# Two transformer blocks in one kernel: the small loads, the output product, the router and the context's channels in another order

## The reference

```python
# first block
h = rmsnorm(x, g_mix)
q_a, k_a, v_a, cx, cb, cc, q_m, gate_logits = split(h @ w_in)      # 768 x 6, 512, 3072 columns
...                       # rope and dilated attention, a convolution, attention to 256 memory rows
merged = sum(sigmoid(gate) * (branch @ w_proj))                    # three branches
x = x + merged @ w_out                                             # 1024 x 1024
h2 = rmsnorm(x, g_ffn)
pg = softmax(h2 @ w_rg + b_rg)                                     # 4 groups, the best one
pe = softmax(the 8 logits of that group)                           # the best 2 experts
weights = pg_top * pe_top / sum(pe_top)
x = x + sum over the picks of weights * (silu(h2 @ w_gate[e]) * (h2 @ w_up[e])) @ w_down[e]   # 32 experts, 512 wide
# second block, with a context of 256 further tokens
mod_c, mod_l = silu(c_ctx) @ w_ada + b_ada, silu(c) @ w_ada + b_ada
pc = project(ctx * (1 + scale_c) + shift_c)     # w_in: channels, conv of 5 taps, silu; gates
pl = project(x * (1 + scale_l) + shift_l)
y, o = SSD scan and gated delta rule, both directions, the context first, its state handed to x
x = layer_norm(alpha * x + g1 * (concat(y, o) @ w_out))
x = layer_norm(alpha * x + g2 * swiglu(x * (1 + scale2) + shift2))
```

## Time and profile before

| | |
|---|---|
| median of three runs | 1622.11 us |
| the three runs | 1621.21, 1622.11, 1624.6 us |
| profiled execution, own time | 1621.47 us |
| its span in the trace | 1619.7 us |
| TensorE's mean granted clock | 0.977 |
| TensorE busy | 1510.5 us |
| VectorE busy | 775.4 us |
| ScalarE busy | 377.3 us |
| GpSimd busy | 217.1 us |
| moved by the DMA engines | 370.46 MB, mean 229 GB/s |

### The profile page before, as it was taken

The page is one execution under the profiler, slowest core; times in us unless marked ns, Lnnn a source line. Parts: engine busy times, 40 slices in busy tenths (PEclk is TensorE's granted clock), DMA queues, the critical chain, the costliest instruction groups (busy, mean ns, idle before and its releaser), DMA issues.

```text
span 1619.7 us, 23438 instructions
## 1 busy us (share of the span) xinstructions
PE 1510.5 (93%) x9510; PEld 1071.4 (66%) x9510; DVE 775.4 (48%) x1583; ACT 377.3 (23%) x842; POOL 217.1 (13%) x364
## 2 busy tenths in 40 slices
PE   7999999999899888779998989999899999999997
PEld 4888655554677565456675768875568774788843
DVE  5557311432544425514445347777987761210156
ACT  1001154321421112223332232133444320100000
POOL 3000000000000000123134010001265612400000
PEclk9999999999999989989999999999999999999999
DMA  9444432653699999999999943342153242444351
GB/s 323 160 156 156 156 104 104 219 194 152 263 406 406 407 406 405 416 418 416 407 417 415 381 165 129 131 156 104 53 221 105 105 156 104 156 156 156 109 203 52
DMA packets 124208, 370.46 MB, mean 229 GB/s; under 512 B 10555, under 2 KB 26565, under 8 KB 107589
## 3 DMA queue, kind: packets, MB, share of 16 engines
q1 hardware_dynamic: 118352, 362.04, 59.1%
q0 software_dynamic: 1280, 6.29, 1.1%
q10 hardware_dynamic: 4469, 0.62, 0.3%
HBM read 367.89 MB, written 1.05 MB: 228 GB/s over the span
## 4 chain that ended last, share of the span: by engine, by line
PE 74%; DMA 10%; DVE 7%; ACT 3%; issue 2%; POOL 2%; ACTq 1%; SPq 1%; DVEq 0%; POOLq 0%
PE psum L2309 49%; PE psum L684 8%; PE psum L2104 4%; DMA ring<-in_w_up 4%; DMA ring<-in_w_in 4%; PE psum L2303 3%; DMA ring<-in_w_down 2%; PE psum L2126 2%; PE psum L2088 1%; PE psum L2145 1%; ACTq L2616 1%; POOL area L1901 1%; PE psum L2475 1%; PE psum L2447 1%; POOL area L1902 1%
## 5 line engine op out<-in xcount | busy, mean ns | idle before, releaser
L2309 PE MATMUL psum<-area,ring 128*128 128x256 f32 (+1 forms) x1952 | 423.2, 376 | 6.4 <-DMA ring<-in_w_in 4.7
L2309 PEld LDWEIGHTS psum<-area,ring 128*128 128x128 f32 x1952 | 361.0, 192 | 57.7 <-DMA ring<-in_w_in 7.0
L2309 PE MATMUL psum<-ring,area 128*128 128x512 f32 (+1 forms) x976 | 386.6, 552 | 9.6 <-ACT area L2600 5.0
L2309 PEld LDWEIGHTS psum<-ring,area 128*128 128x128 f32 x976 | 186.1, 193 | 192.3 <-issue 181.2
L684 PE MATMUL psum<-area 128*128 128x128 f32 x1216 | 152.6, 284 | 15.9 <-DVE area L1493 11.7
L684 PEld LDWEIGHTS psum<-area 128*128 128x128 f32 x1216 | 144.5, 196 | 31.9 <-DVE area L1493 13.1
L2600 ACT ACTIVATE area<-psum 128x512 f32<-128x512 f32 (+1 forms) x103 | 57.0, 586 | 424.5 <-PE psum L2309 354.2
L2104 PE MATMUL psum<-ring,area 128*32 128x256 f32 x1792 | 111.1, 394 | 16.4 <-DMA ring<-in_w_up 16.4
L2309 PE MATMUL psum<-area 128*128 128x256 f32 (+4 forms) x442 | 99.5, 375 | 3.7 <-DVE area L1582 2.6
L2303 PE MATMUL psum<-const,area 128*128 128x128 f32 (+2 forms) x507 | 79.0, 281 | 20.5 <-DVE area L2259 5.5
L2104 PEld LDWEIGHTS psum<-ring,area 128*32 128x32 f32 x1792 | 56.9, 112 | 60.9 <-issue 28.9
(11 more groups left out here) (364 smaller groups left out, 1562.3 us busy)
## 6 DMA issues: line engine op xcount, KB each, us to landing
ring<-in_w_in SPq DMA_DIRECT2D x28, 2048.0 KB, 8.6
ring<-in_w_gate SPq DMA_DIRECT2D x56, 1024.0 KB, 13.5
ring<-in_w_up SPq DMA_DIRECT2D x56, 1024.0 KB, 15.6
ring<-in_w_down SPq DMA_DIRECT2D x48, 1024.0 KB, 14.3
ring<-in_w_ada SPq DMA_DIRECT2D x12, 2048.0 KB, 7.9
area<-in_w_down SPq DMA_DIRECT2D x16, 1024.0 KB, 17.7
ring<-in_w_in SPq DMA_DIRECT2D x12, 1024.0 KB, 12.0
ring<-in_w_out SPq DMA_DIRECT2D x6, 2048.0 KB, 7.7
```

Source lines behind the costliest of these rows:

```text
L2309: last = nc.tensor.matmul(dst, lhs(k), rhs(k), start=first and k == 0, stop=final and k == count - 1)
```

## The change

Six edits, all of order:

1. ScalarE issues the first eight small loads, then does the copies of in0 and the first copies of groups 0 and 1, and then issues the other eight small loads.
2. `v_rest` is put in bank 0 by name, outside the rotation.
3. The output product goes by token tiles: both weight halves for token tile 0, then both for tile 1, with tile 0's eight transposes of h2 between the last two. VectorE and ScalarE follow: add, square sum, root, scale and transposes' copies for each token tile by itself. `wo0` is released after the third tile, not after the second.
4. The context's channel 0 moves from ahead of the h2 transposes to behind the router's transposes.
5. VectorE does the rank's copy and the places before the picks' weights, not behind them.
6. `CTX_GAP` goes from 3 to 1: channels 1 and 2 are woven in among the experts, and the plan of the stage and the list of the weights are made anew from that.

```diff
-CTX_GAP = 3
+CTX_GAP = 1
...
             w, = unit("in4")
-            dst = open_tile("v_rest")
+            dst = open_tile("v_rest", (0,))
...
-            for i in range(2):
-                w, = unit(f"wo{i}")
-                for t in range(NT):
-                    tokens_by_weights(("wo", i, t), mergedT, t, w)
-                used(f"wo{i}")
-
-
-            columns_landed(pe, 0)
-            decay_columns_pe(pe, 0, open_tile, product)
-            context_channel_pe(pe, 0, open_tile, unit, product)
-            for t in range(NT):
+            def turn_h2(t):
                 pe.wait_ge(s["h2_ready"], t + 1)
                 for half in range(2):
                     transposes(("h2T", t, half), [h2[:, t, (4 * half + j) * P:(4 * half + j + 1) * P] for j in range(4)])
+
+            wo = [unit(f"wo{i}")[0] for i in range(2)]
+            for i in range(2):
+                tokens_by_weights(("wo", i, 0), mergedT, 0, wo[i])
+            for i in range(2):
+                tokens_by_weights(("wo", i, 1), mergedT, 1, wo[i])
+                used(f"wo{i}")
+                if i == 0:
+                    turn_h2(0)
+
+
+            columns_landed(pe, 0)
+            decay_columns_pe(pe, 0, open_tile, product)
+            turn_h2(1)
...
-            for n in range(1, CTX_GAP):
-                context_channel_pe(pe, n, open_tile, unit, product)
+            context_channel_pe(pe, 0, open_tile, unit, product)
             pe.wait_ge(s["picked"], NT)
...
-            for dst, src in small_loads:
+            for dst, src in small_loads[:8]:
+                eng.dma_start(dst, src).then_inc(s["small_in"], 16)
+            def first_copy(u):
+                copy_out(("seven", u, 1), partial_sums[u % 2][0], HALF)
+
+            for t in range(NT):
+                copy_out(("in", 0, t), qk[:, t, 0:8, :])
+            for u in range(2):
+                first_copy(u)
+            for dst, src in small_loads[8:]:
                 eng.dma_start(dst, src).then_inc(s["small_in"], 16)
...
-            root(stats[:, 4:6])
-            decay_columns_act(eng, 0)
-            pad_in_act(eng, 0, 0)
-            for t in range(NT):
+            for t in range(NT):
+                root(stats[:, 4 + t:5 + t])
+                if t:
+                    decay_columns_act(eng, 0)
                 for half in range(2):
                     copy_out(("h2T", t, half), h2T[:, 4 * half:4 * half + 4, t * P:(t + 1) * P])
...
-            for n in range(1, CTX_GAP):
-                pad_in_act(eng, 0, n)
+            pad_in_act(eng, 0, 0)
...
-            for i in range(2):
-                for t in range(NT):
+            eng.wait_ge(s["wide_in"], 16)
+            for t in range(NT):
+                for i in range(2):
                     key = ("wo", i, t)
                     part = x[:, t, i * WIDE:(i + 1) * WIDE]
                     v.tensor_tensor(part, wait_filled(eng, key), part, ALU.add).then_inc(drain_of(key), 1)
-
-
-            for i in range(2):
-                for t in range(NT):
+                for i in range(2):
                     wait_drained(eng, ("wo", i, t))
-            for t in range(NT):
                 square_sums(x[:, t, :], h2[:, t, :], stats[:, 4 + t:5 + t])
-            root_mean(stats[:, 4:6], D)
-            eng.wait_ge(s["wide_in"], 16)
-            for t in range(NT):
+                root_mean(stats[:, 4 + t:5 + t], D)
...
+            src = wait_filled(eng, "rank")
+            v.tensor_copy(r_rank.rearrange("p a e -> p (a e)"), src[:, 0:96]).then_inc(drain_of("rank"), 1)
+            wait_drained(eng, "rank")
+            link(v.scalar_tensor_tensor(r_slot, r_pick.rearrange("p t g e -> p t (g e)"), -UNPLACED, r_rank[:, 0:NT, :], ALU.mult, ALU.add))
+            by_slot = lambda rows: rows.rearrange("p (e c) -> p e c", c=CAP)
+            for t in range(NT):
+                v.tensor_tensor(by_slot(place[:, t, :]), slot_row[:, 0:CAP].unsqueeze(1).to_broadcast([P, EXPERTS, CAP]),
+                                spread(r_slot[:, t, :], EXPERTS, CAP), ALU.is_equal).then_inc(s["place_ready"], 1)
+            eng.wait_ge(s["gate_exp"], 1)
+            link(v.tensor_reduce(r_col[:, 2, :], r_tmp[:, 0, :, 0:4], AX.X, ALU.add))
+            link(v.reciprocal(r_col[:, 2, :], r_col[:, 2, :]))
```

23 lines of the change are left out of this document (7 added, 16 removed).

## The result

The changed kernel takes 1627.25 us (median of 17 runs, 1625.81 to 1635.18), the kernel before 1622.11 beside it (17 runs). The ratio, estimated over all these runs, is 1.0039, 95% interval 1.0029 to 1.0049, or 4.7 to 7.9 us; the two medians lie 5.1 us apart, a quotient of 1.0032, inside that interval. The forecast was 1621.4, no change: what came is a small loss clear of noise. The time stands inside the stated range (1616.5 to 1627.5), at its upper end, and the sign was given a chance of 0.25. The profiled execution of the changed kernel took 1626.59 us, span 1624.9, against 1621.47 and 1619.7: 5.2 us of span to explain.

The account below looks back on a forecast made before the run. The prediction took TensorE's chain to bound the front and router, the weight stream the expert stage: -6.1 + 7.3 - 1.9 = -0.7 us on 1621.5, so 1620.8 profiled, 1621.4 beside the median; range 1616.5 to 1627.5.

Parts of the forecast that it names:

- nothing has slack until 927 us: Expert stage: behind the stretch up to channel 1, each microsecond lost is one of the whole time.
- Step 1: Front: eight small loads issued behind the first copies remove TensorE's wait and the slow clock, -5.2 us.
- rival C: Front: the small loads alone are late, 2.8 us; +2.1 in total, 1624.2; chance 0.10.
- Step 2: Front: v_rest in bank 0 removes TensorE's wait at 70.13, -1.6 us; the shifted rotation costs +0.7 at 122.23.
- Step 3: Output product, router and ranks: the new order starts the first gather at 415.3 instead of 419.55, -4.25 us.
- Step 4: Expert stage: channels 1 and 2 among the experts delay the weight stream; last weight 934.4 against 927.1, +7.3 us.
- Step 5: End of expert stage: second half of expert 29's gate and up covers part of TensorE's delta-rule wait, -1.9 us.
- rival B: Expert stage: after 700 us TensorE's work, not the weight landings, sets the pace; -5.1 us, 1617.0; chance 0.18.
- the context stands one piece later: Expert stage until about expert 28: TensorE is delayed mid-stage but not at its end, landings cover it, 0.
- Block 2: Second block: same instructions with banks turned, 0, within 1 us either way.
- rival A: Between h2 transposes and channel 1: short waits lower TensorE's clock, the stream restarts later; +5.1 us, 1627.2; chance 0.22.

Follow-up runs that it names:

- e11_m3_back: The changed kernel with the product M of the delta rule's chunk 3 again ahead of the second half of expert 29: 1631.19 us, ratio 1.0050.
- e2_gap1_only: The kernel before with CTX_GAP = 1 alone, everything else as before: 1636.49 us, ratio 1.0085.
- e3_gap3: The changed kernel with CTX_GAP = 3, channels 0, 1 and 2 behind the router's transposes: 1620.46 us, ratio 0.9980.
- e6_banks: The changed kernel with three places skipped in the rotation of the six banks where the second block begins: 1625.75 us, ratio 1.0019.
- e4_slots: The changed kernel with each load taking the usable slot whose last user is through first in the plan: 1614.02 us, ratio 0.9934.

## Why the prediction was wrong

**What bounds the kernel.** Half right. The stream does set the pace from its restart: in twelve kernels 189 or 190 loads follow `gb2` at 2.57 to 2.59 us each, however early it lands; only the one with gap 2 took 2.61. But "nothing has slack until 927 us" was wrong. From 710 to 927 us TensorE waits 0.6 us for weights in the kernel before and 1.9 in the changed one, against 17 to 18 us for VectorE and ScalarE in each, and its own chain sets the pace. The 3.5 us from last landing to use looked like a lead of the stream; it is how far the stream follows TensorE through the slots. e11_m3_back shows it.

**Step 1 and rival C.** Right: -5.2 by the wait and clock, no wait for the small loads. They took 4.4 to 6.1 us to land, more than the 2 and less than the 12.7 considered, and the last was in at 49.0. The whole front gave 7.4 by 122 us, forecast 6.1; 1.3 is the clock of in0's product, at full speed in this execution, and 1.5 was lost again at 326 to 336.

**Step 2.** Right within 0.2: 1.6 forecast, 1.75 measured (6.36 us early at the third group, 8.11 at `v_rest`), and the +0.7 at 122 us came as +0.7. What the rotation does to the second block I put at "0, within 1": it was +1.0 at 1410 and +0.2 at 1549. One bank is v_rest's, two are the channels' that left the rotation.

**Step 3.** Right in size: -4.4 from 366 us to the gather against -4.25. But the credit was misplaced: from the start of the output product to the gather it is 53.4 us with the old order, 52.8 with CTX_GAP = 1 alone (e2_gap1_only), 54.5 with the reordering alone (e3_gap3 less its half clock) and 49.0 with both. The reordering alone loses, CTX_GAP = 1 alone gains 0.6; only together they give the 4.3.

**Step 4.** Right in mechanism, short in size. The places: `da0` 422.8 (422.0), `gb2` 435.4 (433.8). The 0.8 is half of it gather at half clock, and the step from `da0` to `gb2` took 12.65 and not 11.9: TensorE waits 1.01 us for VectorE (L2259) before expert 0's turn, which the sum of products left out. The recorded sum has a slip besides: 933.5 and half a microsecond are 934.0 and not 934.4, so step 4 should read +6.9 and the forecast 1621.0. With some intervals longer than 2.57 the stream was +3.1 late at expert 27 where the forecast had +1.2 (7.3 - 6.1): 1.9 of the miss.

**Step 5.** The 1.9 us were there (5.37 to 3.33; e11_m3_back takes them away again and loses 2.1), but between 707 and 872 us TensorE lost 1.6: +3.1 became +4.7. The waits for `expand` shrank there as rival B said (11.7 to 5.6 us from 710 to 927), and other waits for VectorE took their place:

```profile
717.61 0.47 PE L2303 MATMUL psum<-const,area 128*128 128x128 f32 x1 [5.55 <-DVE area L2259]
...
780.11 3.78 PE L2088 MATMUL psum<-area 128*128 128x128 f32 x16 [5.13 <-DVE area L2239]
```

In the kernel before the first was 3.87 us, and the second did not stand; with the two smaller ones of 2.58 and 1.46 and the 3.70 of the earlier trace rows it had 11.6 us up to 872, the changed kernel 13.0. I had put "the context stands one piece later" at 0, since the landings would cover it; after 707 they cover nothing. Net -0.7 instead of -1.9: 1.2 of the miss.

**Block 2.** Put at 0, measured +2.8: 1.2 by the banks, 1.3 by the decay columns' half clock, 0.3 in small steps at 1096, 1268 and 1327. Banks and small steps stand in the second profile too, to 0.1 us. There the clock cost 1.3 again, but at other places (0.3 less than before at the decay columns, 1.7 more near 976): the places are the execution's, and whether the order of the program has a part in the amount is left open.

The sum: -0.7 + 1.9 + 1.2 + 2.8 = +5.2, the span's difference. It is one execution's; in the second profile the stage gives +4.5, with rival A's half clock in it, and the block 2.8: +7.3.

**Rivals.** A's number (1627.2) is what came, but its mechanism is only a part: its condition was a restart after 425.9, and the restart was at 422.8. In the second profile of the changed kernel the router's product did run at half clock, as A said, and `gb2` was 1.7 later; the restart was at 424.5, still ahead of 425.9. I had set the row at 404.03, at full clock behind a wait of 1.05 us, against it; the row at 395.26 has the same wait and is at half clock, so one row of one execution could not refute A. (The Trainium skill, TensorE: Matmul & The Clock Gate, What's actually happening, has the throttled clock as the default that activity releases; the row at 395.26, 5.30 us, agrees, and the rows at 404.03 and 395.86, 3.62 us behind a wait as long, show that it does not say when the clock falls.) B was right on what bounds the kernel after 700 and wrong on the sign, as what stands ahead of 700 is passed through the stream.

**The steps that failed.** The one whose mechanism was wrong is the first: one bound for the whole stage, read off a mean DMA share of 1.02, when TensorE's chain sets the pace from about 710 us. On it rested the 0 for the context's later pieces, which measured +1.6. It explains 1.2 us of the 5.9 between -0.7 and +5.2. The larger part is terms put too low: the second block at 0, which measured +2.8 (1.2 of it the banks, shown by e6_banks and by the step at 1405 in every profile), and step 4, 1.9 short. That CTX_GAP, and in it the slots of `da0` and `gb2`, takes the gain back was in the forecast, and e2_gap1_only and e4_slots show it; the loss came of what stands around it.

## What to carry to other kernels

Where a queue in order stands at one slot, ask for each load which slot it waits for and when that is free; moving work behind such a load moves the whole stream, and another choice of slots can be worth more than the work moved (1% here with CTX_GAP = 1, 0.1% with 3). A full DMA row over a stage doesn't say that the transfers set its end: exchange or look at one wait of the compute engine near the end, and see whether landings move with it. An edit that takes tiles out of a rotation of banks moves the banks of everything behind it, so count them modulo the rotation. And before a microsecond or two between two profiles is given to an edit, compare the length of the same instructions: half clock at one product made 1.7 of the 1.9 us in e3_gap3.
